# Attention's second pass: the copies of the outputs over the nearest tokens move from VectorE to ScalarE

## The reference

```python
DILATED_PATTERNS = ((128, 1), (512, 4), (2048, 16))
def dilated_attention(q, k, v, q_g, k_g):
    ...
    res = [_dilated_pattern(qh, kh, vh, w, d) for (w, d) in DILATED_PATTERNS]
    m_max = jnp.max(jnp.stack([r[1] for r in res]), axis=0)
    wts = [jnp.exp(r[1] - m_max) for r in res]
    num = sum(wi[..., None] * r[0] for wi, r in zip(wts, res))
    den = sum(wi * r[2] for wi, r in zip(wts, res))
    out = num / den[..., None]
```

## Time and profile before

| | |
|---|---|
| median of 3 runs | 3051.91 us (3048.99 to 3056.54) |
| time of the profiled execution | 3054.88 us |
| its span in the profile | 3053.2 us |
| mean granted clock of the matrix engine | 0.982 |
| matrix engine busy | 2936.0 us, 96% |
| VectorE busy | 1998.4 us, 65% |
| ScalarE busy | 1147.7 us, 38% |
| GpSimd busy | 283.2 us, 9% |

### The profile page before, as it was taken

The page is one execution under the profiler, slowest core; times in us unless marked ns, Lnnn a source line. Parts: engine busy times, 40 slices in busy tenths (PEclk is TensorE's granted clock), DMA queues, the critical chain, the costliest instruction groups (busy, mean ns, idle before and its releaser), DMA issues. The chain is left out here.

```text
span 3053.2 us, 38696 instructions
## 1 busy us (share of the span) xinstructions
PE 2936.0 (96%) x14818; PEld 2308.2 (76%) x14818; DVE 1998.4 (65%) x2490; ACT 1147.7 (38%) x1734; POOL 283.2 (9%) x280
## 2 busy tenths in 40 slices
PE   7999999997989999899999999899999999999999
PEld 5778887874657566688778888788888788877887
DVE  7334555117575755445598899889998786776743
ACT  6332121212434444311255544554444444444321
POOL 0000000003434343000001000000000000000000
PEclk9999999998999999999999999999999999999999
DMA  4552222226774755543422234525543666453632
GB/s 146 173 187 56 73 71 62 86 75 186 198 189 142 214 141 148 168 154 133 148 104 83 97 121 159 196 83 185 195 158 104 235 206 220 161 154 113 193 115 67
DMA packets 260089, 435.02 MB, mean 142 GB/s; under 512 B 44014, under 2 KB 128494, under 8 KB 252878
## 3 DMA queue, kind: packets, MB, share of 16 engines
q1 hardware_dynamic: 255534, 408.32, 42.4%
q0 software_dynamic: 4384, 24.41, 2.2%
HBM read 312.18 MB, written 120.00 MB: 142 GB/s over the span
## 5 line engine op out<-in xcount | busy, mean ns | idle before, releaser
L103 PE MATMUL up_banks<-up_x_hi,up_w_hi 128*128 128x512 f32 x1232 | 484.8, 394 | 23.4 <-DVE up_x_lo L2677 8.4
L104 PE MATMUL up_banks<-up_x_lo,up_w_hi 128*128 128x512 f32 x1232 | 482.6, 392 | 0.0
L105 PE MATMUL up_banks<-up_x_hi,up_w_lo 128*128 128x512 f32 x1232 | 482.2, 391 | 0.0
L103 PE MATMUL inp_ps<-inp_h_hi,carry_q 128*128 128x512 f32 x896 | 353.3, 394 | 13.4 <-DVE inp_h_lo L202 9.5
L104 PE MATMUL inp_ps<-inp_h_lo,carry_q 128*128 128x512 f32 x896 | 350.2, 391 | 0.0
L105 PE MATMUL inp_ps<-inp_h_hi,carry_k_two 128*128 128x512 f32 x896 | 350.0, 391 | 0.0
L103 PEld LDWEIGHTS up_banks<-up_x_hi,up_w_hi 128*128 128x128 f32 x1232 | 233.0, 189 | 78.6 <-issue 15.7
L105 PEld LDWEIGHTS up_banks<-up_x_hi,up_w_lo 128*128 128x128 f32 x1232 | 233.2, 189 | 48.8
L104 PEld LDWEIGHTS up_banks<-up_x_lo,up_w_hi 128*128 128x128 f32 x1232 | 233.3, 189 | 48.4 <-issue 0.2
L103 PE MATMUL down_banks<-down_x_hi,down_w_hi 128*128 128x512 f32 x616 | 241.2, 392 | 7.4 <-DVE down_x_lo L2189 7.4
L2718 DVE SCALAR_TENSOR_TENSOR carry_rows<-carry_squares,up_conv_w,carry_rows 128x1024 f32<-128x1024 f32 x176 | 232.2, 1319 | 24.3 <-ACT carry_rows L2549 19.4
(11 more groups left out here) (378 smaller groups left out, 5373.3 us busy)
## 6 DMA issues: line engine op xcount, KB each, us to landing
carry_room<-in_w_up_dram SPq DMA_DIRECT2D x84, 512.0 KB, 4.4
act<-carry_rows SPq DMA_DIRECT2D x44, 512.0 KB, 2.9
carry_room<-cum_rows SPq DMA_DIRECT2D x16, 1024.0 KB, 6.7
carry_room<-x SPq DMA_DIRECT2D x7, 2048.0 KB, 9.3
carry_room<-in_w_in_dram SPq DMA_DIRECT2D x26, 512.0 KB, 5.9
xbc<-carry_room SPq DMA_DIRECT2D x12, 1024.0 KB, 5.7
carry_room<-xbc SPq DMA_DIRECT2D x16, 768.0 KB, 4.8
down_x<-act SPq DMA_DIRECT2D x12, 1024.0 KB, 8.3
```

The costliest lines, as they stand in the source:

```text
L103: pe.matmul(out, w_hi, x_hi, start=first, stop=False, skip_group_check=onto)
L104: pe.matmul(out, w_hi, x_lo, start=False, stop=False, skip_group_check=onto)
L105: return pe.matmul(out, w_lo, x_hi, start=False, stop=last, skip_group_check=onto)
```

## The change

ScalarE takes outputs 0 to 7 of each head out of PSUM, in the new function `first_add`, by two activations of 128x256 with the function Copy in every head. Each pair is issued behind an exponential: pair j behind exponential 2j+3 for j from 0 to 6, pair 7 behind exponential 16. The waits for the stores of the head before, or for its scores, go along, and the first pair of heads 1 to 3 also waits for all takings-out of the head before (`o_add`). VectorE keeps outputs 8 to 23; its first addition of a head waits for `o_add` of the eight pairs.

```diff
@@ -1016,6 +1016,10 @@
                 bank = self.banks[:, g % 2].rearrange("p (h b t) -> p h b t", h=2, b=2)
                 blocks = slice(0, 2 if follows or k >= 2 * TT else 1)
                 act.activation(self.probs[:, g % self.RING, :, blocks], bank[:, :, blocks], ACT.Exp).then_inc(self.exp_s, 1)
+                if k < TT and k % 2 and k > 2:
+                    self.first_add(act, r, k // 2 - 1)
+                if k == TT:
+                    self.first_add(act, r, 7)
 
     def vector(self, dve):
         yield self.at(1, 0, -0.5)
@@ -1034,7 +1038,8 @@
                 if h == 0 and r == KVH - 2:
                     dve.wait_ge(self.a_mm, self.FIRST * KVH)
                     dve.memset(self.q1[HD:HD + 1, :].bitcast(F32), 1.0).then_inc(self.ones_s, 1)
-                self.add(dve, r, h)
+                if h >= 8:
+                    self.add(dve, r, h)
                 if h == self.VALUES // 2:
                     if r + 1 < KVH:
                         self.negate(dve, r + 1)
@@ -1097,21 +1102,9 @@
         h = r * self.VALUES + j
         bank = self.banks[:, 2 + h % 2].rearrange("p (w t) -> p w t", w=2)
         dve.wait_ge(self.pv_mm, h + 1)
-        if j < 8:
-            if j == 0 and r == KVH - 1:
-                dve.wait_ge(self.s_mm, self.STEPS * r)
-            elif j == 0 and r > 0:
-                dve.wait_ge(self.den_in, 32 * r)
-                dve.wait_ge(self.o_st, 16 * r)
-            if r == KVH - 1:
-                for w, into in enumerate(self.result(r)):
-                    last = dve.tensor_copy(into[:, self.run(0, 2 * j, 2)].rearrange("p (x i) -> p i x", i=RES),
-                                           bank[:, w].rearrange("p (i x) -> p i x", i=RES))
-                last.then_inc(self.o_add, 1)
-            else:
-                dve.tensor_copy(self.o_den[:, :, self.run(0, 2 * j, 2)].rearrange("p w (x i) -> p w i x", i=RES),
-                                bank.rearrange("p w (i x) -> p w i x", i=RES)).then_inc(self.o_add, 1)
-        elif j < 16:
+        if j == 8:
+            dve.wait_ge(self.o_add, h)
+        if j < 16:
             if r == KVH - 1:
                 for w, into in enumerate(self.result(r)):
                     into = into[:, self.run(1, 2 * j - TT, 2)]
@@ -1125,6 +1118,23 @@
             bank = bank.rearrange("p w (i t) -> p w i t", i=2)
             dve.tensor_tensor(out, bank[:, 0], out, ALU.add)
             dve.tensor_tensor(den[0:2 * 32], bank[0:2 * 32, 1], den[0:2 * 32], ALU.add).then_inc(self.o_add, 1)
+
+    def first_add(self, act, r, j):
+
+        h = r * self.VALUES + j
+        bank = self.banks[:, 2 + h % 2].rearrange("p (w t) -> p w t", w=2)
+        act.wait_ge(self.pv_mm, h + 1)
+        if j == 0 and r == KVH - 1:
+            act.wait_ge(self.s_mm, self.STEPS * r)
+        elif j == 0 and r > 0:
+            act.wait_ge(self.den_in, 32 * r)
+            act.wait_ge(self.o_st, 16 * r)
+        if j == 0 and r > 0:
+            act.wait_ge(self.o_add, h)
+        for w, into in enumerate(self.result(r)):
+            last = act.activation(into[:, self.run(0, 2 * j, 2)].rearrange("p (x i) -> p i x", i=RES),
+                                  bank[:, w].rearrange("p (i x) -> p i x", i=RES), ACT.Copy)
+        last.then_inc(self.o_add, 1)
 
     def inverses(self, dve):
         for r in range(KVH):
```

## The result

The changed kernel takes 3060.80 us (median of 20 runs, 3056.14 to 3067.43) against 3052.16 us (median of 20) before: ratio 1.0030, 95% interval 1.0024 to 1.0036, slower by 8.6 us by the medians and 9.2 us by the ratio. Forecast were 3064.6 us (+12.7) and a range of 3054 to 3073. The profiled execution has a span of 3059.5 us.

What follows compares the result with a forecast made beforehand. The matrix engine was taken as the bound. Blocked bursts (+11.0) and one clock drop (+1.7) on 3054.88 gave 3067.6 us profiled, 3064.6 as median; range 3060 to 3069, or 3054 to 3073 with the cheap price and clock case.

Steps and rivals of the forecast that it cites:

- The bound: Whole kernel: the matrix engine, busy 2936.0 of 3053.2 us, sets the time; taking 36 us off VectorE gains 0.
- The price: ScalarE's 64 strided activations: 0.62 us each was taken, with 0.376 us for a dense write as the lower value.
- the turn of a pair: Time two copies hold ScalarE: 1.04 us at the upper price, 0.56 us at the lower.
- The bursts: Six stretches of state-space work on ScalarE where copies delay exponentials: 11.0 us lost in all, 3.7 in the worst.
- the sixth: Last head's first burst of state-space work on ScalarE: a loss of 0.15 us.
- the two prices of the forecast: A copy on ScalarE at 0.62 us (total loss 11.0 us) or at 0.376 us (6.3 us).
- The forecast's lower price: Copies at the dense 0.376 us, a pair 0.56 us: total loss 6.3 us, 2.7 of it in the worst burst.
- The clock: Last head, behind the new 2.7 us wait before scores 19: one drop to the 1.2 GHz level, +1.7 us.
- Cheap copies: Rival: ScalarE writes the stride at the dense price, +6.3 us, about 3058 us; chance 0.19.
- Hidden anyway: Rival: the exponentials regain their lead in slack and nothing changes, 3052 us; chance 0.15.
- Faster: Rival: less VectorE work removes the matrix engine's 7.5 us of waits for state additions, at best 3044 us; chance 0.04.
- More clock drops: Rival: each of three blocked bursts costs a clock drop, +5 to +9 on the 11, about 3071 us; chance 0.12.

Runs made afterwards that it cites:

- dve_load: Changed kernel, plus VectorE waiting for the same outputs and reducing a constant tile in place of each moved copy; ratio 1.0026 to the kernel before.
- dense: Changed kernel, but ScalarE writes the 256 outputs side by side in place of every fourth element; ratio 1.0023 to the kernel before.
- last_head: Kernel before, with only the last head's eight pairs of copies moved to ScalarE; ratio 1.0007 to the kernel before.
- wait_only: Kernel before, copies left on VectorE; ScalarE only waits for the outputs where the changed kernel has its copies; ratio 1.0010.
- all_late: Changed kernel, but every copy j stands one group of scores later, behind exponential 2j+5; ratio 1.0007 to the kernel before.

## Why the prediction was right

**The bound.** Right: the matrix engine's busy time is the same to 0.1 us, and the time moved by its waits. VectorE's 33 us less gained nothing (dve_load).

**The price.** The instruction was taken at 0.62 us and took 0.65; the stride was the reason (dense: 0.38). The remark on 16-byte lines in the Trainium skill ("SBUF — State Buffer", section "Door 1: The DMA port swizzle") says that an access which goes to a new line each time pays a penalty; this pair of numbers agrees with it, though no run here tries another stride. The term that was mis-sized is the turn of a pair: I had 1.04 us, with an overlap of 0.1 us as between dense activations. The changed kernel's timeline of ScalarE gives it, start of a pair to start of what follows:

```profile
934.89 1.11 ACT L1135 ACTIVATE mix_o_den<-mix_a_banks 128x256 f32<-128x256 f32 x2 [1.90 <-PE mix_a_banks L1317]
935.77 1.24 ACT L1489 ACTIVATE carry_room<-carry_room,carry_cum 128x128 f32<-128x128 f32 x4
...
940.14 1.07 ACT L1135 ACTIVATE mix_o_den<-mix_a_banks 128x256 f32<-128x256 f32 x2
940.99 0.64 ACT L1018 ACTIVATE mix_probs<-mix_a_banks 128x512 f32<-128x512 f32 x1
```

935.77-934.89 = 0.88 and 940.99-940.14 = 0.85 us: two strided activations overlap their neighbours by some 0.2 us each.

**The bursts.** All five that were given more than 0.2 us show, and the sixth shows nothing. By the starts: first head 0.7 us (forecast 1.1), second 1.2 (2.1), third 1.5 and 2.4 (1.5 and 2.5), last 0 and 4.1 with its clock drop (0.15 and 3.7+1.7). Together 9.9 us for 12.7. With the turn of 0.87 us put between the two prices of the forecast, its own sum is, as an estimate, 6.3 + (0.87-0.56)/(1.04-0.56) x 4.7 = 9.3 us in place of 11.0, or 11.0 with the clock. Most of the 1.1 us that are left is a second term, one that was put too small. In the bursts the matrix engine of the kernel before waited for the state three times, 0.25, 0.26 and 0.56 us (the forecast read "about 0.3 us each"); in the changed kernel the state products come later and all three are gone: 1.1 us, of which the forecast had taken off 0.25. The longest of the three, and then another wait of the kernel before:

```profile
1186.36 0.67 PE L1646 MATMUL mix_ps_x<-mix_xde,mix_b_tok 128*128 128x512 f32 x1 [0.56 <-DVE mix_state L1563]
...
913.91 0.96 PE L1646 MATMUL mix_ps_x<-mix_xde,mix_b_tok 128*128 128x512 f32 x1 [1.29 <-DVE mix_state L1563]
```

The second, of 1.29 us, makes up the rest of the fall from 7.5 to 5.1 us. It lies in a first pass, and last_head, which changes nothing ahead of the last head, lacks it too: it is not the change's. The turn and the state waits both made the forecast too high; its sum was not right by one error cancelling another.

**Waiting against occupying.** The forecast's lower price left most of the loss, as the wait for outputs stays; that is what dense and wait_only show. Without the 0.9 us before scores 3, waiting alone adds 3.3 us of wait for exponentials (1.0010) and occupying alone (all_late) 1.1 us (1.0007, with 1.3 us of wait for the state); both together add 8.1 us, more than the 4.4 us of the two (5.7 with the wait for the state). That both use up the same slack would explain it; I have not tested this. The forecast's sentence that copy 7 is done before VectorE's first addition needs it held in the changed kernel; in the three kernels with late copies it does not.

**The clock.** The drop in the last head came, at the place named. Windows of the changed kernel: the wait, the stretch behind it, and then the 2 us without work near 1014 us and the stretch behind that one:

```profile
1189.00:1191.30 2.30, 0.03 (x1) 0.03 (x2) 2.15 (x3) 2.30 (x8) 0.00 (x0) 1.00 0.00 0
1193.00:1196.40 3.40, 3.40 (x21) 1.47 (x11) 1.90 (x3) 1.60 (x3) 2.33 (x3) 0.51 0.00 0
1014.30:1016.50 2.20, 0.22 (x2) 0.13 (x2) 1.69 (x3) 0.00 (x0) 1.96 (x2) 1.00 0.90 196
1016.50:1020.00 3.50, 3.50 (x34) 2.40 (x34) 2.43 (x3) 0.00 (x0) 3.42 (x3) 1.00 0.93 245
```

The first wait is followed by a clock of 0.51. The second, of the same length as that of the earlier trace rows, is followed by a full clock here, where before it was 0.51. The stretch behind the wait before scores 19 in dense, in dve_load and in wait_only:

```profile
1188.50:1191.90 3.40, 3.40 (x28) 2.05 (x28) 1.32 (x2) 3.02 (x5) 1.02 (x1) 0.50 0.00 0
...
1199.40:1202.80 3.40, 3.40 (x14) 1.60 (x7) 2.02 (x3) 1.38 (x3) 2.54 (x4) 0.50 0.00 0
...
1179.70:1183.10 3.40, 3.38 (x31) 1.99 (x32) 2.31 (x3) 3.31 (x6) 0.74 (x1) 1.00 0.00 0
```

Over all ten profiles: at this place the clock fell in each of the four with a wait of 2.0 to 2.4 us (changed, dve_load, last_head, dense) and in none of the six with 1.5 us or less. Near 1013 us, behind an idle of 1.96 to 2.01 us that all ten have, it fell in five of ten. So the forecast's drop came where it was put, but the one row it was taken from, that of 1013 us, shows a place where it comes as often as not: in part this was luck.

Such drops differ from profile to profile all through the kernel. By the starts the changed profile is 0.1 us behind at 778 us, 10.1 us at 1240 us and 6.3 us at the end; the 3.8 us in between are not the change's. The bursts' 9.9 us and the 8.6 us between the medians are the numbers to compare.

**The rivals.** Cheap copies: refuted by the 652 ns. Hidden anyway: refuted by 10.2 us of waits. Faster: refuted, and in dve_load the load given back cost nothing that shows. More clock drops: one came behind these waits, not three. By size the result lies at 0.3%, just where slower was told from no change; the ratio's interval does not settle on which side of it.

## What to carry to other kernels

An engine that is 38% busy on average can be full for the ten microseconds in which the new work is due; read its load in the stretches where the work will stand, not over the span. Before an instruction that waits for another engine is put into an in-order queue, list what stands behind it: here, by the medians of the ratios, a wait without any work cost a third of the loss, and one group later in the queue took away three quarters of it. Then list who waits for the instruction that you put later: here VectorE's first addition did, and in its queue the block came back. Taking load off an engine is worth something only if the bound waits for it.

## What was not expected of the hardware

Activations that write every fourth f32 (16 bytes apart) overlap their neighbours more than dense ones do: a pair of 0.65 us each takes a turn of 0.85 to 0.88 us, a dense pair of 0.38 us each 0.54 us. And the same idle of about 2 us of the matrix engine, near 1013 us, was followed by 3.4 us at the lower clock in five profiles and by none in the five others, while a wait of 2.0 to 2.4 us before scores 19 of the last head was followed by it in four of four.
